# Memory keys and values in halves between the attention's steps, the first query piece by token halves, convolution taps by channel pairs

## What is computed

```
def hybrid_mixer(x, ...):
    proj = x @ w_in + b_in
    c_q, c_kv, k_r, u = proj[..., :256], proj[..., 256:512], proj[..., 512:544], proj[..., 544:]
    y_att = mla_group(c_q, c_kv, k_r, ...)       # 8 heads, rms norm of c_q and c_kv, rotary part from k_r
    y_conv = conformer_conv_group(u, ...)        # a * sigmoid(g), 31 causal taps per channel, layer norm, silu
    return jnp.concatenate([y_att, y_conv], axis=-1) @ w_o

def memory_cross_attention(x, mem, w_q, w_kv, w_o):
    q = (x @ w_q).reshape(B, S, 4, 256)
    kv = (mem @ w_kv).reshape(B, M, 2, 4, 256)   # 256 memory rows, the same in both layers
    ...softmax over the memory, weighted values...
    return o @ w_o

for l in range(2):
    x = layer_norm(ALPHA * x + hybrid_mixer(x, ...), ln1)
    x = layer_norm(ALPHA * x + memory_cross_attention(x, mem, ...), ln2)
    x = layer_norm(ALPHA * x + swiglu_ffn(x, ...), ln3)
```

## Time and profile before

| | us |
|---|---|
| median of 3 runs (lowest, highest) | 3740.95 (3739.96, 3743.77) |
| the profiled execution | 3747.37 |
| its span, first to last instruction | 3745.5 |
| PE busy | 3326.5 (89%) |
| DVE busy | 1323.0 (35%) |
| ACT busy | 873.1 (23%) |
| first block, both layers | about 0 to 1420 |

### The profile page before, as it was taken

The page is one execution under the profiler, slowest core; times in us unless marked ns, Lnnn a source line. Parts: engine busy times, 40 slices in busy tenths (PEclk is TensorE's granted clock), DMA queues, the critical chain, the costliest instruction groups (busy, mean ns, idle before and its releaser), DMA issues.

```text
span 3745.5 us, 35516 instructions
## 1 busy us (share of the span) xinstructions
PE 3326.5 (89%) x14976; PEld 2239.5 (60%) x14976; DVE 1323.0 (35%) x2235; ACT 873.1 (23%) x1375; POOL 161.3 (4%) x146
## 2 busy tenths in 40 slices
PE   6878989999977889999899998899699899898994
PEld 4437668887635667888688876677533333333332
DVE  3365353334267444333533443633411111111112
ACT  2332223222233232222223342122111111111111
POOL 0110000000010000000110101000100000000001
PEclk8988999999988999999899999999799999999997
DMA  3102312323201312233221222022489999999996
GB/s 133 35 1 79 112 57 85 100 86 113 92 0 45 101 57 79 94 103 104 76 69 56 81 79 69 29 79 90 162 360 423 422 423 423 423 422 422 423 420 254
DMA packets 225012, 625.41 MB, mean 167 GB/s; under 512 B 14768, under 2 KB 128176, under 8 KB 175696
## 3 DMA queue, kind: packets, MB, share of 16 engines
q1 hardware_dynamic: 203216, 579.37, 40.2%
q10 hardware_dynamic: 19440, 35.58, 2.7%
q0 software_dynamic: 2192, 8.13, 0.7%
HBM read 600.23 MB, written 22.81 MB: 166 GB/s over the span
## 4 chain that ended last, share of the span: by engine, by line
PE 67%; DMA 16%; DVE 10%; ACT 3%; POOL 2%; issue 2%; ACTq 0%; DVEq 0%; POOLq 0%
PE bank L120 65%; DMA piece<-in_moe_w 3%; DMA piece_high<-in_moe_w 3%; DMA mT_slot<-in_moe_w 3%; DMA xT<-in_moe_w 2%; PE bank L123 2%; DVE gate_acc L138 2%; DMA norm_room<-in_moe_w 1%; POOL root L135 1%; DMA memT<-in_moe_w 1%; DVE x_tok L138 1%; DMA y_att_slot<-in_moe_w 1%; DVE stat L153 1%; DVE probs L141 1%; POOL raw_q L135 1%
## 5 line engine op out<-in xcount | busy, mean ns | idle before, releaser
L120 PE MATMUL bank<-xT_rounded,piece_high_rounded 128*128 128x512 f32 (+1 forms) x1376 | 543.6, 395 | 25.5 <-DVE xT_low_rounded L135 13.6
L135 DVE TENSOR_TENSOR piece_rounded<-piece,piece_high_rounded 128x2048 fp32r<-128x2048 f32 (+1 forms) x156 | 342.1, 2198 | 630.4 <-ACT piece_high_rounded L126 630.2
L120 PE MATMUL bank<-xT_low_rounded,piece_high_rounded 128*128 128x512 f32 (+1 forms) x1376 | 533.6, 388 | 0.0
L120 PE MATMUL bank<-xT_rounded,piece_rounded 128*128 128x512 f32 (+1 forms) x1376 | 533.3, 388 | 0.0
L135 DVE TENSOR_TENSOR gate_and_hidden<-gate_and_hidden,bank 64x512 f32<-64x512 f32 x64 | 69.1, 1080 | 844.7 <-ACT gate_and_hidden L126 844.7
L126 ACT ACTIVATE piece_high_rounded<-piece 128x2048 fp32r<-128x2048 f32 (+1 forms) x156 | 283.1, 1821 | 291.2 <-DMA piece<-in_ffn_w_down 116.2
L120 PEld LDWEIGHTS bank<-xT_rounded,piece_high_rounded 128*128 128x128 f32 x1376 | 262.6, 191 | 84.3 <-DVE xT_low_rounded L135 14.4
L120 PEld LDWEIGHTS bank<-xT_low_rounded,piece_high_rounded 128*128 128x128 f32 x1376 | 262.7, 191 | 54.6 <-issue 4.1
L120 PEld LDWEIGHTS bank<-xT_rounded,piece_rounded 128*128 128x128 f32 x1376 | 262.2, 191 | 52.5
L120 PE MATMUL bank<-piece,xeT 128*64 128x512 f32 x488 | 239.7, 645 | 23.6 <-DMA norm_room<-in_moe_w 8.4
L120 PE MATMUL bank<-piece_high,xeT 128*64 128x512 f32 x464 | 184.6, 628 | 15.4 <-DMA piece<-in_moe_w 10.7
(11 more groups left out here) (331 smaller groups left out, 5149.7 us busy)
## 6 DMA issues: line engine op xcount, KB each, us to landing
piece<-in_moe_w SPq DMA_DIRECT2D x90, 1024.0 KB, 17.0
piece_high<-in_moe_w SPq DMA_DIRECT2D x88, 1024.0 KB, 17.1
xT<-in_moe_w SPq DMA_DIRECT2D x59, 1024.0 KB, 17.0
mT_slot<-in_moe_w SPq DMA_DIRECT2D x58, 1024.0 KB, 17.3
piece<-in_ffn_w_in SPq DMA_DIRECT2D x40, 1024.0 KB, 5.2
memT<-in_moe_w SPq DMA_DIRECT2D x30, 1024.0 KB, 16.2
y_att_slot<-in_moe_w SPq DMA_DIRECT2D x30, 1024.0 KB, 16.9
norm_room<-in_moe_w SPq DMA_DIRECT2D x29, 1024.0 KB, 17.1
```

Of the source, the lines that this page charges most:

```text
L120: return self.engine.matmul(*a, **k) if self.engine is not None else Nothing()
L135: return self.engine.tensor_tensor(*a, **k) if self.engine is not None else Nothing()
```

## The change

- The key-rope product moves behind the first gate and input pieces, its swap behind all four; the convolution projections go by channel pairs (gate 0, in 0, gate 1, in 1). Taps go by channel pairs too: 4 behind the first pair, 12 ahead of the second pair's products on VectorE, then 4 in each step instead of 3 (so they end with step 27).
- The memory keys and values leave their places. Values are now pieces of 256 columns like the keys. Each of the 32 steps gets, behind its scores, one half of a 256-column product (4 matmuls): values in steps 0 to 15, keys in steps 16 to 31. ScalarE copies a result in each odd step. Values go first to `mem_v_early`, in the later room of the query's low part, and are moved by a transfer of 1 MB once the latents are done with; keys lie in the room of the norm parameters, and the mixer's norm parameters get a room of their own.
- In the output projection the first piece waits only for the attention's outputs; the way back of the convolution result (`z_back`) stands behind that piece, and the second piece waits for it.
- The first piece of the cross query is done by halves of 256 tokens, as the first piece of the feed-forward already was, with the turning of the last tile between them.

```diff
@@ pieces
-            by_columns("conv gate", w, U0 + CONV, U0 + 2 * CONV)
-            by_columns("conv in", w, U0, U0 + CONV)
+            for c0 in range(0, CONV, 2 * P):
+                by_columns("conv gate", w, U0 + CONV + c0, U0 + CONV + c0 + 2 * P)
+                by_columns("conv in", w, U0 + c0, U0 + c0 + 2 * P)
+            by_columns("memory values", a["xa_w_kv"][layer], D, 2 * D, wants_split=False)
             by_columns("memory keys", a["xa_w_kv"][layer], 0, D, wants_split=False)
             for half in range(2):
                 by_rows("mix out", a["mix_w_o"][layer], 0, KD, half * BANK, (half + 1) * BANK)
-            for half in range(2):
-                by_rows("memory values", a["xa_w_kv"][layer], 0, KD, D + half * BANK, D + (half + 1) * BANK,
-                        wants_split=False)
@@ project_out_pe
                 self.release(e, n)
+                if behind_first and not half and not k0:
+                    behind_first()
@@ mixer_pe (kr moved behind the first pair, kr_swap behind both)
-        for label, done in (("conv gate", "gate"), ("conv in", "h")):
-            for c in range(0, CT, 2):
+        for c in range(0, CT, 2):
+            for label, done in (("conv gate", "gate"), ("conv in", "h")):
...
@@ mixer_pe, in a step
                 banks.give(("s", l, n), "masked", l, n)
+                if n < 16:
+                    self.half_values_pe(e, l, n)
+                else:
+                    self.half_keys_pe(e, l, n - 16)
@@
+    def half_values_pe(self, e, layer, u):
+
+        q, m, k0 = u // 4, u // 2 % 2, u % 2 * (KD // 2)
+        if u % 4 == 0:
+            self.values_piece = self.pe_piece(e, "memory values")
+        n = self.values_piece
+        if u % 2 == 0:
+            self.banks.take(e, "mem_v", layer, q, m)
+        e.wait_ge(*self.piece_ready(n))
...
+        self.product(e, self.bank("mem_v", layer, q, m)[:, 0:2 * P],
+                     lambda k: self.memT[:, k0 + k, m * P:(m + 1) * P], lambda k: cols(k0 + k), KD // 2,
+                     first=(k0 == 0), last=(k0 > 0)).then_inc(*e.tick("pe", "mem_v", layer, q, m, k0))
@@ mixer_act, in a step
+            if n < len(steps) and n % 4 == 0:
+                self.act_piece(e, "memory values" if n < 16 else "memory keys")
+            if n < len(steps) and n % 2:
+                if n < 16:
+                    self.values_act(e, l, n // 4, n // 2 % 2)
+                else:
+                    self.keys_act(e, l, n // 2 - 8)
@@ mixer_dve
-        taps = iter([(j, c4) for j in range(TAPS) for c4 in range(CT)])
+        taps = iter([(j, c4) for c in range(0, CT, 2) for j in range(TAPS) for c4 in (c, c + 1)])
...
-            self.convolve(e, l, taps, 3)
+            self.convolve(e, l, taps, 4)
@@ cross_pe
         self.project_out_pe(e, f"mix{l}", "mix out", KD,
...
-                            [("y_split", l, k) for k in range(CT)] + [("z_split", l, k) for k in range(CT)],
-                            lambda i: self.rows_to_T_pe(e, f"xT_mix{l}", i, self.x_tok, f"mix{l}", "normed", i))
+                            lambda k0: [("z_split" if k0 else "y_split", l, k) for k in range(CT)],
+                            lambda i: self.rows_to_T_pe(e, f"xT_mix{l}", i, self.x_tok, f"mix{l}", "normed", i), z_back)
...
+            if j == 0:
+                two = [banks.take(e, "xq", l, c) for c in both]
+                for _ in self.two_by_halves_pe(e, n, two, f"xT_mix{l}", [("pe", "xq", l, c) for c in both]):
+                    self.rows_to_T_pe(e, f"xT_mix{l}", NT - 1, self.x_tok, f"mix{l}", "normed", NT - 1)
...
-                e.wait_ge(*at("mem_v", l, 1, MT - 1))
+                e.wait_ge(*at("mem_v_home", l))
@@ cross_act
+        e.wait_ge(*at("pe", "k", l, HEADS - 1))
+        for q in range(4):
+            e.wait_ge(*at("mem_v", l, q, MT - 1))
+        e.dma_start(self.mem_v, self.mem_v_early).then_inc(*e.lands("memory_values_moved", "mem_v_home", l))
+        self.act_piece(e, "mix out")
...
-        before = () if l == 0 else (f"ffn{l - 1}b", "normed", NT - 1)
-        self.load_norm(e, f"mix{l}", a["ln1_g"][l], a["ln1_b"][l], *before)
+        self.load_norm(e, f"mix{l}", a["ln1_g"][l], a["ln1_b"][l], "pe", "y", l, HEADS * NT - 1)
```

More of the change, by code:

```diff
@@ L766, in norm_dve @@
         x = self.x_tok[:, i, :]
+        gain, shift = self.norm_params(key)
         e.wait_ge(*self.at(key, "stats", 1, i))
@@ L945, in mixer_pe @@
                 self.release(e, n)
+            if c == 0:
+                bank = banks.take(e, "kr", l)
+                e.wait_ge(*at("kr_split", l))
+                self.product(e, bank[0:ROPE, :], lambda k: (krh3[:, k, :], kr3[:, k, :]), self.x_all, KD).then_inc(
+                    *e.tick("pe", "kr", l))
+                banks.give(("kr", l), "kr_copied", l)
+        bank = banks.take(e, "kr_swap", l)
+        e.wait_ge(*at("kr_biased", l))
+        e.matmul(bank[NOPE:QKD, :], self.swap_q[NOPE:QKD, NOPE:QKD], kr, start=True, stop=True).then_inc(
+            *e.tick("pe", "kr_swap", l))
+        banks.give(("kr_swap", l), "kr_sin", l)
         if l == 0:
@@ L1009, in mixer_pe, with half_keys_pe @@
                     banks.give(("y", l, h // 2), "y_split", l, h // 2)
+    def half_keys_pe(self, e, layer, u):
+        c, k0 = u // 2, u % 2 * (KD // 2)
+        if u % 4 == 0:
+            self.keys_piece = self.pe_piece(e, "memory keys")
+        n = self.keys_piece
+        if u % 2 == 0:
+            self.banks.take(e, "mem_k", layer, c)
+        e.wait_ge(*self.piece_ready(n))
+        for m in range(MT):
+            e.wait_ge(*self.at("memT", m, 4))
+        cols = self.piece_cols(n, c % 2 * P, P)
+        self.product(e, self.bank("mem_k", layer, c)[:, 0:MEM], lambda k: cols(k0 + k), lambda k: self.memT[:, k0 + k, :],
+                     KD // 2, first=(k0 == 0), last=(k0 > 0)).then_inc(*e.tick("pe", "mem_k", layer, c, k0))
+        if k0:
+            self.banks.give(("mem_k", layer, c), "mem_k", layer, c)
+        if u % 4 == 3:
+            self.release(e, n)
@@ L1194, in cross_pe @@
         l, banks, at = layer, self.banks, self.at
-        for j in range(KD // 2):
-            n = self.pe_piece(e, "memory keys")
-            for c in (2 * j, 2 * j + 1):
-                bank = banks.take(e, "mem_k", l, c)
-                e.wait_ge(*self.piece_ready(n))
-                for m in range(MT):
-                    e.wait_ge(*at("memT", m, 4))
-                self.product(e, bank[:, 0:MEM], self.piece_cols(n, (c - 2 * j) * P, P), lambda k: self.memT[:, k, :],
-                             KD).then_inc(*e.tick("pe", "mem_k", l, c))
-                banks.give(("mem_k", l, c), "mem_k", l, c)
-            self.release(e, n)
         for i in range(NT):
@@ L1225, in cross_pe @@
-        for half in range(2):
-            for m in range(MT):
-                banks.take(e, "mem_v", l, half, m)
-            for k0 in (0, KD // 2):
-                n = self.pe_piece(e, "memory values")
-                for m in range(MT):
-                    e.wait_ge(*self.piece_ready(n))
-                    self.product(e, self.bank("mem_v", l, half, m)[:, :],
-                                 lambda k: self.memT[:, k0 + k, m * P:(m + 1) * P], self.piece_cols(n, 0, BANK), KD // 2,
-                                 first=(k0 == 0), last=(k0 > 0)).then_inc(*e.tick("pe", "mem_v", l, half, m, k0))
-                    if k0:
-                        banks.give(("mem_v", l, half, m), "mem_v", l, half, m)
-                self.release(e, n)
@@ L1359, in cross_dve @@
         l, at = layer, self.at
-        for j in range(KD // 2):
-            self.dve_piece(e, "memory keys")
-            self.convolve(e, l, self.taps, 6)
         self.convolve(e, l, self.taps, CT * TAPS)
@@ L1382, in turned @@
                 self.rows_to_T_dve(e, f"xT_mix{l}", i - 2, self.xT, self.xT_low)
-        self.project_out_dve(e, f"mix{l}", "mix out", KD, ALPHA, True, x_from, turned)
-        for half in range(2):
-            self.dve_piece(e, "memory values")
-            self.dve_piece(e, "memory values")
+        self.project_out_dve(e, f"mix{l}", "mix out", KD, ALPHA, True, x_from, turned, begun=1)
         for i in range(2, NT):
```

158 lines of the change are left out of this document (88 added, 70 removed).

## The result

| | before | after |
|---|---|---|
| median of the runs, us | 3742.36 (3739.96 to 3746.04) | 3609.7 (3607.44 to 3613.43) |
| ratio, 95% interval | | 0.9646, 0.9629 to 0.9662 |
| span of the profiled execution, us | 3745.5 | 3609.8 |
| first instruction of cross out, layer 0 / layer 1, us | 504.4 / 1398.7 | 432.3 / 1261.4 |

What follows compares the result with a forecast made beforehand. In the first block DMA is no bound; in attention no engine is full, a softmax chain passing round. Gains less costs of 66.6 us a layer, 133 for two, take 3747.4 to 3614, median 3608; range 3586 to 3655.

Steps and rivals of the forecast that it cites:

- Part 1: Latents to attention: moved key-rope product and swap, and split pieces, take 50.0 us instead of 60.0; gain 10.0 a layer.
- Part 2: Attention: 55.1 us of memory products added, old work 110 to 93 by clock, stage 154.8 against 147.6; cost 7.
- Part 3: Memory keys: their separate TensorE stretch leaves the path; gain 27.5 us a layer.
- Part 4: Convolution result to output projection's first half: first weight piece covers VectorE's normalising, 42.4 to 32.6 us; gain 9.8.
- Part 5: Output projection's end without values takes 31.6 us against 59.5, gain 27.9; query's first piece by halves costs 1.4.
- rival 5: Kernel's end: saving is taken back because experts wait for DMA anyway; no change, 3741 us; chance 0.02.
- the bound of 23.6: Attention: the most us its old TensorE work could win back from the low clock level; forecast took 17.
- rival 2: Attention: clock stays at its present mean, cost 34 us a layer in place of 7; 3662 us; chance 0.09.
- 3 (nothing hides): Rival 3, attention: none of the added products hides, cost 55 us a layer; 3704 us; chance 0.04.
- Rival 1: Attention: VectorE in step with TensorE, fourth tap adds to the period, 18 us worse a layer; 3644 us; chance 0.12.
- my own spread: Whole kernel: forecast's own range 3588 to 3632 us, from an attention cost of -3.6 to +16 a layer.

Runs made afterwards that it cites:

- e5: Changed kernel with the rotary key's product and swap ahead of the convolution's gates again, as in the kernel before; 3627.23 us.
- e1: Changed kernel with the 32 half products of memory keys and values behind the attention's steps instead of between them; 3732.95 us.
- e3: Changed kernel with each half product between the attention's steps computed twice into the same sum; 3705.14 us.
- e6: Changed kernel with the convolution result's transposes back ahead of the first output piece again; 3617.49 us.
- e7: Changed kernel with the first cross query piece computed for all 512 tokens at once instead of by halves; 3612.13 us.
- e9: Changed kernel with convolution pieces and taps in the order of the kernel before, no taps ahead of the attention; 3622.97 us.
- e10: As e8, with VectorE's rounding of the query's first piece behind the second tile's norm instead of ahead of the first tile; 3597.68 us.
- e11: Changed kernel with four useless products in the gaps of the cross attention's last three steps; 3604.18 us.
- e12: Changed kernel with the edits of e10 and e11 together; 3596.31 us.
- e2: As e1, with half as many useless products at the half products' old places between the attention's steps; 3716.97 us.
- e4: Changed kernel with six convolution taps behind each attention step instead of four; 3625.03 us.
- e8: Changed kernel with both output projection pieces needing only attention's result first, then the two for the convolution's result tile by tile; 3603.7 us.

## Why the prediction was right, step by step

The gains and costs a layer, in us, from the profiled executions, each at the same edge in both:

| step | forecast | layer 0 | layer 1 | shown by |
|---|---|---|---|---|
| ahead of the latents' last matmul | 0 | gain 1.2 | cost 0.4 | - |
| Part 1, latents to attention | gain 10.0 | 9.8 | 8.7 | e5: 9.6, 9.1 |
| Part 2, attention | cost 7.2 | 1.3 | 5.7 | e1 to e3 |
| Parts 3 and 4, keys and convolution result | gain 37.3 | 37.5 | 37.4 | e6 for the z way |
| Part 5, values and halves | gain 26.5 | 26.5 | 26.8 | e7 for the halves |
| cross attention | 0 | cost 1.7 | cost 1.7 | open |
| sum | 66.6 | 72.0 | 65.1 | |

The sum of both layers is 137.1, forecast 133. 1.4 us were lost again between layer 1's cross out and the feed-forward, and the expert stage moved as a block (rival 5 is out): the spans differ by 135.7. That the median came within 2 us of the forecast is in part luck: the attention cost 5.9 and 1.5 us less than forecast, and the cross attention, Part 1 of layer 1 and the feed-forward took most of that back.

**Part 1.** As forecast: 50.1 us from the latents' last matmul to the end of the key's swap where I had 50.0. The gain is the cover for two waits, not the pairs of pieces: e5 gives it back with the pairs in place, e9 keeps it without them. The 1.2 us ahead of it can't be put down to the change: that edge lies between 59.8 and 61.4 us in the profiles of after and of the twelve runs.

**Part 2.** The mechanism was right: TensorE sets the pace, with heads 18.4 us apart in the mean of layer 0 where I had 18.5, and its old work runs at the higher of its two levels, 2.4 GHz. The term was mis-sized by a few us: TensorE's work was 142.9 and 144.6 us where I had 148, and its idle time 6.1 as forecast (6.7). So of the old work's 110 and 108 us some 22 and 19 came back, not 17, near the bound of 23.6 that I had worked out. In e5, e6, e10, e11 and e12, whose steps are untouched, the stage took 150.6 or 150.7 us in layer 0, so after's 149.0 there is the low end, and 3 us is the fairer cost. The difference is the first unit, behind the wait for GpSimd: 1.89 us in after, 3.2 to 3.6 in those five. Of rival 2 (the clock stays) and 3 (nothing hides), the dose series says why they failed: the clock is 0.82 with the gaps and 1.00 with the units, and the idle time falls from 46.0 to 6.1 us. The Trainium skill (TensorE: Matmul & The Clock Gate, "A second HAM failure mode: psum-queue depth-cycling") speaks of swinging between both levels for such a cycle of banks; the trace agrees for e1 (0.82) and, in two heads, for e2 (0.96), and not for after, which stays at 1.00 with 6.1 us of pauses in all. Rival 1 (VectorE in step) is out at four taps (TensorE waits 0.9 us for them) and comes in in part at six (e4) or where a split stands ahead of taps (e9). I had priced the place of the taps only in sum; that they end (16 early ones and four in each of the first 27 steps) before the split at step 28 was luck in my reasoning, and worth 12 us.

**Part 3.** Gone, as forecast.

**Part 4.** Start of the second piece at +19.6 us, forecast +19.7 (the terms that I gave, 12.8 + 6.3, make 19.1; the prediction gives no source for the other 0.6); first half done at +32.4, forecast +32.6. The wait left over was 5.0 us, about as the prediction said, and e8 and e10 show that it could be covered.

**Part 5.** 31.1 us for a stretch that I took as 31.6 from the cross stage. The query's first piece took 14.4 us, forecast 14.3, at 0.86 of the clock; another 0.4 to 0.8 us were lost behind it. What the halves hide is nearly what they cost, so e7 finds little.

**Not in the sum.** The cross attention's 1.7 us.

**Slips without weight.** The DMA digits stand at 9 from the thirty-first slice on, not the thirtieth. A cost of 16 us in the attention gives 3626, not the 3632 of my own spread. The pauses ahead of the fall of the clock in the earlier trace rows were one of 0.3 and one of 1.9 us, not several of 1 to 2.

## What to carry to other kernels

Where the granted clock of a stage is between its two levels, price its fill by the stage's own work at the upper level plus the fill, and compare with the idle time: here 55 us of needed work went into stages of 147.6 and 145.0 us for 1.3 and 5.7. Try it with a half dose of useless work first, which needs no new data flow: if the stage gets shorter, the clock was the cost. When an engine takes side work in a chain (taps), look at where it stands relative to each piece that the engine may have to wait for, not only at its sum; and order weight pieces by which operand is ready, not by which output they make.

## What was unexpected of the hardware

- A stage got 5.0 to 6.7 us shorter by 55 us more TensorE work (155.7 to 150.7 or 149.0), and 9.5 shorter by half of that.
- The same four waits of 0.3 to 0.9 us ahead of the same eight instructions gave 5.40 us in one layer and 3.70 in the other of the same execution (e9).
- Useless products in gaps of about their own length cost nothing measurable (e12 against e10, 3596.3 and 3597.7).
